# A mixture-of-experts loop: the next expert's gather moved from behind the down projection into it

## The chip, the cores and the metric

The kernel runs on one core of a Trainium2 chip. The metric is the device time of one execution in microseconds (us). All data are float32. TensorE is called PE in the profile, VectorE DVE, ScalarE ACT, GpSimd POOL, SyncE SP.

## The reference, cut to what matters

Two layers over 256 latent tokens of width 1024. The change touches only the last sub-layer, a top-2-of-8 expert SwiGLU (each expert 1024 to 3584 to 1024):

```python
def moe_swiglu(h, router, w_gate, w_up, w_down):
    logits = (h @ router).astype(jnp.float32)
    probs = jax.nn.softmax(logits, axis=-1)
    vals, idx = lax.top_k(probs, TOP_K)
    wts = vals / jnp.sum(vals, axis=-1, keepdims=True)
    combine = jnp.sum(jax.nn.one_hot(idx, N_EXPERTS, dtype=jnp.float32) * wts[..., None], axis=-2)
    ...
    for e in range(N_EXPERTS):
        out = out + combine[..., e:e + 1] * swiglu(h, w_gate[e], w_up[e], w_down[e])
    return out
```

## The kernel before, in words

**Weights.** All weights come as one stream of 2 MB units. SP sends each into one of seven slots of `ring` and waits for the slot's semaphore `used[s]` before it sends the next unit there. An expert has 21 units: 14 for gate and up, 7 for down.

**The loop.** Since 256 tokens choose two experts each, an expert sees only some of them. The kernel picks a padded width for each expert (64, 96, 128, 144, 160, 192 or 256 tokens) from the counts that it finds at run time. The expert loop is a hardware loop (`pe.Fori(0, E)`), and every engine has its own. Inside it, `for_width` is a ladder of if and else on PE: one *arm* of code for each width. The first arm is width 64, and an expert of width 144 passes three branches to reach the fourth. For this input the widths of the eight experts are 64, 96, 144, 64, 128, 64, 96, 64; they can be read from the tiles of the matmuls (64: 128x64 weights, 96: 128x64 and 128x32, 128 and 144: 128 or 144 moving columns at L1186). So there are seven *crossings* from one expert to the next, called crossing 1 to 7 here; crossing 1 is 64 to 96, 2 is 96 to 144, 3 is 144 to 64, 4 is 64 to 128, 5 is 128 to 64, 6 is 64 to 96 and 7 is 96 to 64.

**One expert on PE.** In the arm: `gate_up` (L1204 for widths 64 and 96, L1186 for wider ones; 14 units, banks 0 to 3 of `ps`), then `down` (L1242; 7 units d = 0 to 6, banks 4 to 7). ACT's silu (L419) and DVE's product (L760, which counts `e_a`) make the input of down; for narrow experts it is turned by L1174 and copied by ACT (L412). Behind the arm, in code that all widths share: `gather(e + 1)` (L1135, 16 matmuls, banks 0 to 3) under `pe.If(e < E - 1)` at L1272, which selects the next expert's tokens with a matrix of zeros and ones; then a second ladder with `combine` (L1260), which adds the expert's result to its tokens: 4 matmuls of 512 columns for one block of up to 128 slots (widths 64 and 128), 8 for two blocks (96 and 144). Then the loop's own branch (L1148) goes back to its head, where PE reads the next width and climbs the ladder.

**Around it.** ACT (L437) and DVE (L767) each copy two banks of down's result to `y_slot`, which combine reads; then both take the gathered columns to `hTe` with scale and shift (L402, L747), which the next gate_up reads; DVE adds combine's result to `y_sum` (L773). The last down unit's slot is released by the first gather matmul.

Of the kernel before, what the change touches and what calls it, by code (L numbers as in the profile page):

```python
# [21 lines left out]
P = 128  # L22
# [14 lines left out]
E = 8  # L37
# [4 lines left out]
RING = 7  # L42
UNIT = 4096
BANK = 512
# [39 lines left out]
BASE = len(ORDER)  # L84
# [12 lines left out]
def build(nc, stream, x_in, ctx_in, vecs, consts, rope, dft, gains, ada_b, norm_w, late, out):  # L97
    ctx = ExitStack()
    with ctx:
# [182 lines left out]
        def _(act):  # L282
# [115 lines left out]
            def take_gather(count):  # L398
                for k in range(KD // 2):
                    if k % 2 == 0:  # L400
                        act.wait_ge(gather_ps, count + k // 2 + 1)
                    act.activation(hTe[:, k, :], ps[:, k // 2, (k % 2) * SEQ:(k % 2 + 1) * SEQ], ACT.Identity,  # L402
                                   bias=ab[:, 4, 1, k:k + 1], scale=ab[:, 4, 0, k:k + 1]).then_inc(hTe_act, 1)
# [3 lines left out]
            with act.Fori(0, E) as e:  # L407
                which = act.value_load(width_at[0:1, bass.ds(e, 1)], min_val=0, max_val=len(WIDTHS))

                def take_turned(u):  # L410
                    act.wait_ge(eT_ps, e * GU_UNITS + u + 1)
                    act.activation(aT_e[:, u, :, :].rearrange("p b n -> p (b n)"), ps[:, 6 + u % 2, :],  # L412
                                   ACT.Copy).then_inc(eT_ok, 1)

                def silu_units(wide):
                    for u in range(GU_UNITS):
                        act.wait_ge(e_ps, e * GU_UNITS + u + 1)
                        q = 2 * (u % 2)
                        act.activation(gated_e[:, u % 2, :, :], ps[:, q:q + 2, 0:SEQ], ACT.Silu).then_inc(e_silu, 1)  # L419
                        if u and not wide:  # L420
                            take_turned(u - 1)
                        if u == 5:
                            act.wait_ge(selT_ps, e + 1)
                            act.activation(selT[:, :, :].rearrange("p b t -> p (b t)"), ps[:, 4, :],
                                           ACT.Copy).then_inc(selT_ok, 1)
                    if wide:
                        act.sem_inc(eT_ok, GU_UNITS)
                    else:
                        take_turned(GU_UNITS - 1)

                with act.If(which < WIDE):
                    silu_units(False)
                with act.If(which >= WIDE):
                    silu_units(True)
                act.wait_ge(ye_ps, e + 1)
                for b in range(2):
                    act.activation(y_slot[:, b, 0:BANK], ps[:, 4 + 2 * b, :], ACT.Copy).then_inc(ye_act, 1)  # L437
                with act.If(e < E - 1):
                    take_gather(e * 4 + 4)

            act.activation(stat[:, 127:128], eps[:, 0:1], ACT.Sqrt)

# [10 lines left out]
        def _(dve):  # L453
# [289 lines left out]
            def take_gather(count):  # L743
                for k in range(KD // 2, KD):
                    if k % 2 == 0:
                        dve.wait_ge(gather_ps, count + k // 2 + 1)
                    dve.tensor_scalar(hTe[:, k, :], ps[:, k // 2, (k % 2) * SEQ:(k % 2 + 1) * SEQ],  # L747
                                      ab[:, 4, 0, k:k + 1], ab[:, 4, 1, k:k + 1], ALU.mult,
                                      ALU.add).then_inc(hTe_dve, 1)
# [4 lines left out]
            with dve.Fori(0, E) as e:  # L754
                dve.wait_ge(gather_ps, e * 4 + 4)
                select(e + 1, False)
                for u in range(GU_UNITS):
                    dve.wait_ge(e_silu, e * GU_UNITS + u + 1)
                    q = 2 * (u % 2)
                    dve.tensor_tensor(aT_e[:, u, :, :], gated_e[:, u % 2, :, :], ps[:, q:q + 2, SEQ:2 * SEQ],  # L760
                                      ALU.mult).then_inc(e_a, 1)
                    if u == 7:
                        dve.wait_ge(selT_ps, e + 1)
                        select(e + 1, True)
                dve.wait_ge(ye_ps, e + 1)
                for b in range(2):
                    dve.tensor_copy(y_slot[:, b, BANK:2 * BANK], ps[:, 5 + 2 * b, :]).then_inc(ye_dve, 1)  # L767
                with dve.If(e < E - 1):
                    take_gather(e * 4 + 4)
                for i in range(4):  # L770
                    dve.wait_ge(comb_ps, e * 4 + i + 1)
                    part = y_sum[:, i // 2, (i % 2) * BANK:(i % 2 + 1) * BANK]
                    dve.tensor_tensor(part, part, ps[:, 4 + i, :], ALU.add).then_inc(comb_ok, 1)  # L773
# [12 lines left out]
        def _(pe):  # L786
# [338 lines left out]
                with pe.Else():  # L1125
                    for_width(which, body, i + 1)

            def gather(e, before=None):

                pe.wait_ge(sel_ok, e + 1)
                for j in range(4):
                    for i in range(2):
                        for b in range(TB):
                            last = pe.matmul(ps[:, j, i * SEQ:(i + 1) * SEQ], xn[:, b, (2 * j + i) * P:(2 * j + i + 1) * P],  # L1135
                                             sel[:, b, :], start=(b == 0), stop=(b == TB - 1))
                            if (j, i, b) == (0, 0, 0) and before is not None:
                                last.then_inc(used[before], 1)
                    last.then_inc(gather_ps, 1)

            def landed_of(e, i):
# [6 lines left out]
            with pe.Fori(0, E) as e:  # L1148
# [74 lines left out]
                def down(width):  # L1223
                    pe.wait_ge(selT_ok, e + 1)
                    done, count = done_before(width, GU_UNITS), 0
                    for d in range(NFE // 4):
                        s = landed_of(e, GU_UNITS + d)
                        pe.wait_ge(e_a if is_wide(width) else eT_ok, e * GU_UNITS + 2 * d + 2)
                        w = ring[:, s, :].rearrange("p (f n) -> p f n", f=4)
                        for b, (s0, n) in enumerate(BLOCKS[width]):  # L1230
                            tiles = P // n
                            if d == 0 and b == 1 and not is_wide(width):
                                pe.wait_ge(eT_ok, (e + 1) * GU_UNITS)
                            for h in range(2):
                                for f in range(4):
                                    j, r = 4 * d + f, f % tiles
                                    u = j // 2 if tiles < 4 else 2 * d + 1
                                    c = n * (f % 2 if tiles < 4 else f)
                                    a_T = aT_e[:, u, b, c:c + n]
                                    if is_wide(width):  # L1240
                                        a_T = aT_e[:, j // 2, j % 2, s0:s0 + n]
                                    last = pe.matmul(ps[n * r:n * (r + 1), 4 + 2 * b + h, :], a_T,  # L1242
                                                     w[:, f, h * BANK:(h + 1) * BANK],
                                                     start=(j < tiles), stop=(j >= NFE - tiles))
                                    if count < len(done):
                                        last.then_inc(used[(BASE + done[count]) % RING], 1)
                                    count += 1
                            if d < NFE // 4 - 1 and b == len(BLOCKS[width]) - 1:
                                last.then_inc(used[s], 1)
                            if d == 0 and b == 0 and not is_wide(width):  # L1250
                                turn(width, GU_UNITS - 1)
                    last.then_inc(ye_ps, 1)
                    if is_wide(width):
                        pe.sem_inc(eT_ps, GU_UNITS)

                def combine(blocks):

                    for i in range(4):
                        for b in range(blocks):
                            last = pe.matmul(ps[:, 4 + i, :], selT[:, b, (i // 2) * P:(i // 2 + 1) * P],  # L1260
                                             y_slot[:, b, (i % 2) * BANK:(i % 2 + 1) * BANK],
                                             start=(b == 0), stop=(b == blocks - 1))
                        last.then_inc(comb_ps, 1)

                def expert(width):
# [3 lines left out]
                pe.wait_ge(hTe_act, e * 4 + 4)  # L1269
                pe.wait_ge(hTe_dve, e * 4 + 4)  # L1270
                for_width(width, expert)
                with pe.If(e < E - 1):  # L1272
                    gather(e + 1, (BASE + PER_EXPERT - 1) % RING)
                pe.wait_ge(ye_act, e * 2 + 2)
                pe.wait_ge(ye_dve, e * 2 + 2)
                for_width(width, lambda w: combine(len(BLOCKS[w])))
# [97 lines left out]
```

## Time and profile before

| | before |
|---|---|
| median of 3 runs | 1636.34 us (1633.12 to 1638.41) |
| the profiled execution | 1634.14 us, of which the span is 1632.4 us |
| mean granted clock of TensorE | 0.968 of full speed |
| PE busy | 1524.1 us, 93% of the span |
| DVE, ACT busy | 381.2 us (23%), 266.3 us (16%) |
| moved by DMA | 474.35 MB, mean 291 GB/s |

The span is the time from the first to the last instruction that the profiler recorded; 1.7 us of the execution lie around it. [...] "Issue" in a row is idle time of an engine in which it waited for nothing that the profile shows as work.
### The profile page before, as it was taken

To read this page: it belongs to the slowest core of one execution; us is meant where nothing else is said; L and a number is where in the kernel's file an instruction comes from. 1 tells how busy PE (TensorE), PEld (TensorE's weight loads), DVE (VectorE), ACT (ScalarE), POOL (GpSimd) and SP (SyncE) were. 2 spreads that over 40 slices of the span, in tenths; PEclk is the share of its full clock that TensorE was granted. 3 is DMA by queue.
4 is the path that set the end of the run, shared out by engine and by line. 5 is a ranking of instruction groups with operands and counts; after the bars stand their busy time and mean duration, and the time that the engine had idled before them with its cause. 6 is when DMAs were issued, how large, how long until landed. Compare 5 with 4: busy or idle time off the path is not lost.

```text
span 1632.4 us, 22184 instructions
## 1 busy us (share of the span) xinstructions
PE 1524.1 (93%) x9552; PEld 980.6 (60%) x9553; DVE 381.2 (23%) x663; ACT 266.3 (16%) x506; POOL 16.6 (1%) x18
## 2 busy tenths in 40 slices
PE   5999999999999799799879999996999998999897
PEld 3445598864686464454369954545995564553462
DVE  2668514400265421110010100211010120110212
ACT  3235210001100222121100001221000131120122
POOL 1000010000000000000000000000000000000000
PEclk7999999999999799899989999998999999999999
DMA  9863176842687269889827766798878699889595
GB/s 388 339 255 139 71 291 253 301 187 82 253 316 302 108 283 426 375 339 373 371 75 262 274 244 232 303 428 358 295 287 303 243 428 427 358 350 407 227 428 243
DMA packets 34239, 474.35 MB, mean 291 GB/s; under 512 B 3824, under 2 KB 4112, under 8 KB 5696
## 3 DMA queue, kind: packets, MB, share of 16 engines
q1 hardware_dynamic: 32800, 467.90, 72.2%
q0 software_dynamic: 1024, 3.38, 0.6%
q8 instruction: 120, 1.97, 0.5%
q10 hardware_dynamic: 288, 1.05, 0.2%
q14 instruction: 7, 0.06, 0.0%
HBM read 471.26 MB, written 1.05 MB: 289 GB/s over the span
## 4 chain that ended last, share of the span: by engine, by line
PE 84%; DMA 7%; issue 4%; DVE 4%; ACT 1%; SPq 0%; DVEq 0%
PE ps L1204 22%; PE ps L1186 13%; PE ps L1242 13%; PE ps L997 9%; PE ps L974 8%; DMA ring<-stream 7%; PE ps L1048 5%; PE ps L1135 4%; PE ps L843 3%; PE ps L1260 2%; PE ps L1174 1%; DVE acc L511 1%; DVE att L574 1%; PE ps L945 0%; PE ps L1219 0%
## 5 line engine op out<-in xcount | busy, mean ns | idle before, releaser
L1204 PE MATMUL ps<-ring,hTe 128*64 128x256 f32 (+1 forms) x3584 | 361.8, 384 | 11.3 <-issue 9.9
L1204 PEld LDWEIGHTS ps<-ring,hTe 128*64 128x64 f32 (+1 forms) x3584 | 216.6, 131 | 134.4 <-issue 27.3
L1242 PE MATMUL ps<-ring,aT 128*64 128x512 f32 (+2 forms) x1232 | 286.7, 597 | 7.9 <-DMA ring<-stream 6.4
L1186 PE MATMUL ps<-hTe,ring 128*128 128x144 f32 (+1 forms) x1792 | 215.2, 284 | 20.9 <-issue 20.9
L1186 PEld LDWEIGHTS ps<-hTe,ring 128*128 128x128 f32 x1792 | 214.6, 194 | 22.7 <-issue 22.7
L1242 PEld LDWEIGHTS ps<-ring,aT 128*64 128x64 f32 (+2 forms) x1232 | 96.2, 139 | 188.0 <-issue 170.7
L760 DVE TENSOR_TENSOR aT<-hT,ps 128x512 f32<-128x512 f32 x112 | 77.0, 687 | 548.0 <-ACT hT L419 548.0
L419 ACT ACTIVATE hT<-ps 128x512 f32<-128x512 f32 x112 | 66.9, 597 | 569.5 <-PE ps L1204 337.1
L997 PE MATMUL ps<-hT,ring 128*128 128x256 f32 (+1 forms) x832 | 153.4, 347 | 0.0
L997 PEld LDWEIGHTS ps<-hT,ring 128*128 128x128 f32 x832 | 138.1, 191 | 15.7 <-issue 1.0
L511 DVE SCALAR_TENSOR_TENSOR acc<-ring,silu_c,acc 128x1024 f32<-128x1024 f32 (+1 forms) x92 | 105.2, 1143 | 2.0
L974 PE MATMUL ps<-ring,aT 128*128 128x512 f32 x240 | 104.5, 594 | 0.0
L1135 PE MATMUL ps<-acc,xn 128*128 128x256 f32 x256 | 68.3, 433 | 23.4 <-issue 20.7
L1048 PE MATMUL ps<-hT,ring 128*128 128x256 f32 (+1 forms) x480 | 83.9, 337 | 0.0
L1048 PEld LDWEIGHTS ps<-hT,ring 128*128 128x128 f32 x480 | 76.2, 191 | 7.9 <-issue 0.5
L1135 PEld LDWEIGHTS ps<-acc,xn 128*128 128x128 f32 x256 | 56.0, 222 | 38.6 <-issue 26.6
L974 PEld LDWEIGHTS ps<-ring,aT 128*128 128x128 f32 x240 | 45.1, 190 | 56.2 <-issue 56.2
L767 DVE COPY acc<-ps 128x512 f32<-128x512 f32 x16 | 10.3, 686 | 286.4 <-PE ps L1242 286.4
L412 ACT ACTIVATE aT<-ps 128x512 f32<-128x512 f32 x84 | 49.8, 593 | 18.2 <-PE ps L1174 18.2
L437 ACT ACTIVATE acc<-ps 128x512 f32<-128x512 f32 x16 | 8.7, 594 | 257.0 <-PE ps L1242 257.0
L843 PE MATMUL ps<-ring,hT 128*128 128x512 f32 x96 | 43.1, 610 | 1.3 <-DVE hT L498 1.3
L1260 PE MATMUL ps<-acc 128*128 128x512 f32 x88 | 39.2, 593 | 1.6 <-DVE acc L767 1.6
(180 smaller groups left out, 705.1 us busy)
## 6 DMA issues: line engine op xcount, KB each, us to landing
ring<-stream SPq DMA_DIRECT2D x222, 2048.0 KB, 11.1
gg<-norm_w POOLq DMA_DIRECT2D x4, 512.0 KB, 14.8
x<-x_in SPq DMA_DIRECT2D x1, 1024.0 KB, 5.1
hTe<-ctx_in SPq DMA_DIRECT2D x1, 1024.0 KB, 7.9
out<-x ACTq DMA_DIRECT2D x2, 512.0 KB, 2.6
aT<-dft POOLq DMA_DIRECT2D x1, 512.0 KB, 10.8
aT<-rope POOLq DMA_DIRECT2D x1, 256.0 KB, 15.4
acc<-late POOLq DMA_DIRECT2D x1, 192.0 KB, 2.7
```

The lines of the kernel that those rows point to most:

```text
L419: act.activation(gated_e[:, u % 2, :, :], ps[:, q:q + 2, 0:SEQ], ACT.Silu).then_inc(e_silu, 1)
L511: last = dve.scalar_tensor_tensor(out=dst, in0=slot(what)[:, k * D:(k + 1) * D][:, cols], scalar=silu_c[:, 4 * h + k, 0:1], in1=dst, op0=A ...
L760: dve.tensor_tensor(aT_e[:, u, :, :], gated_e[:, u % 2, :, :], ps[:, q:q + 2, SEQ:2 * SEQ], ALU.mult).then_inc(e_a, 1)
L843: last = pe.matmul(ps[:, blk, :], lhs[:, k, b * P:(b + 1) * P], w[:, k, :], start=(k == 0), stop=(k == KD - 1))
L974: last = pe.matmul(ps[:, 4 + 2 * b + h, :], lhs(k)[:, b * P:(b + 1) * P], w[:, k % per_unit, h * BANK:(h + 1) * BANK], start=(k == 0), sto ...
L997: last = pe.matmul(ps[:, j % 4, g * SEQ + t0:g * SEQ + t1], w[:, j % 2, g, k, :], hT[:, k, t0:t1], start=(k == 0), stop=(k == KD - 1))
L1048: last = pe.matmul(ps[:, bank, c + t0:c + t1], w[:, i % 4, k, :], hT[:, k, t0:t1], start=(k == 0), stop=(k == KD - 1))
L1135: last = pe.matmul(ps[:, j, i * SEQ:(i + 1) * SEQ], xn[:, b, (2 * j + i) * P:(2 * j + i + 1) * P], sel[:, b, :], start=(b == 0), stop=(b = ...
L1186: last = pe.matmul(ps[:, 2 * (u % 2) + b, g * SEQ:g * SEQ + width], w, hTe[:, k, 0:width], start=(k == 0), stop=(k == KD - 1))
L1204: last = pe.matmul(to, hTe[:, k, s0:s0 + n], w, start=(k == 0), stop=(k == KD - 1))
L1242: last = pe.matmul(ps[n * r:n * (r + 1), 4 + 2 * b + h, :], a_T, w[:, f, h * BANK:(h + 1) * BANK], start=(j < tiles), stop=(j >= NFE - tiles))
L1260: last = pe.matmul(ps[:, 4 + i, :], selT[:, b, (i // 2) * P:(i // 2 + 1) * P], y_slot[:, b, (i % 2) * BANK:(i % 2 + 1) * BANK], start=(b = ...
```

## The change

On PE the gather of expert e+1 leaves the shared code. It stands now in each of the seven arms, in `down`, behind the fourth unit (d = 3), under an if of its own that skips it for the last expert. There it waits until all 14 products of the expert are made (`e_a`), since it writes banks 0 to 3. On ACT and DVE the taking of the gathered columns (`take_gather`) goes ahead of the copies of down's result. The slot of the last down unit is now released by the first matmul of combine; so that this comes early, combine's first group of 512 columns is split into 128 and 384.

```diff
@@ ACT (act) @@
+                with act.If(e < E - 1):
+                    take_gather(e * 4 + 4)
                 act.wait_ge(ye_ps, e + 1)
                 for b in range(2):
                     act.activation(y_slot[:, b, 0:BANK], ps[:, 4 + 2 * b, :], ACT.Copy).then_inc(ye_act, 1)
-                with act.If(e < E - 1):
-                    take_gather(e * 4 + 4)
@@ DVE (dve) @@
+                with dve.If(e < E - 1):
+                    take_gather(e * 4 + 4)
                 dve.wait_ge(ye_ps, e + 1)
                 for b in range(2):
                     dve.tensor_copy(y_slot[:, b, BANK:2 * BANK], ps[:, 5 + 2 * b, :]).then_inc(ye_dve, 1)
-                with dve.If(e < E - 1):
-                    take_gather(e * 4 + 4)
@@ PE, down(width) @@
+                        if d == 3:
+                            with pe.If(e < E - 1):
+                                pe.wait_ge(e_a, (e + 1) * GU_UNITS)
+                                gather(e + 1)
                     last.then_inc(ye_ps, 1)
@@ PE, combine(blocks) @@
-                        for b in range(blocks):
-                            last = pe.matmul(ps[:, 4 + i, :], selT[:, b, (i // 2) * P:(i // 2 + 1) * P],
-                                             y_slot[:, b, (i % 2) * BANK:(i % 2 + 1) * BANK],
-                                             start=(b == 0), stop=(b == blocks - 1))
+                        half = slice((i % 2) * BANK, (i % 2 + 1) * BANK)
+                        for part in ([slice(0, P), slice(P, BANK)] if i == 0 else [slice(0, BANK)]):
+                            for b in range(blocks):
+                                last = pe.matmul(ps[:, 4 + i, part], selT[:, b, (i // 2) * P:(i // 2 + 1) * P],
+                                                 y_slot[:, b, half][:, part], start=(b == 0), stop=(b == blocks - 1))
+                                if part.stop == P and b == 0:
+                                    last.then_inc(used[(BASE + PER_EXPERT - 1) % RING], 1)
                         last.then_inc(comb_ps, 1)
@@ PE, the loop @@
                 for_width(width, expert)
-                with pe.If(e < E - 1):
-                    gather(e + 1, (BASE + PER_EXPERT - 1) % RING)
                 pe.wait_ge(ye_act, e * 2 + 2)
                 pe.wait_ge(ye_dve, e * 2 + 2)
                 for_width(width, lambda w: combine(len(BLOCKS[w])))
```

How it stands in the program, on PE at the end of the arm for width 64 (a name like `ps<-ring,aT` is output and inputs; the line number of a row may shift by two to three between the kernels). Before:

```order
L1242 MATMUL ps<-ring,aT 64x512 x40
L1123 UNCONDITIONAL_BRANCH
L1123 COMPARE_AND_BRANCH
L1143 ISA
L1204 MATMUL ps<-ring,hTe 64x2x128 x32
```

And of the change:

```order
L1240 MATMUL ps<-ring,aT 64x512 x16
L1251 COMPARE_AND_BRANCH
L1252 REGISTER_ALU
L1131 REGISTER_ALU
L1135 MATMUL ps<-acc,xn 128x256 x16
L1251 UNCONDITIONAL_BRANCH
L1240 MATMUL ps<-ring,aT 64x512 x24
L1123 UNCONDITIONAL_BRANCH
```

The last 40 down matmuls were one run; now 24 of them follow the gather, and the arm's exit branch follows them as before.

On PE behind the ladder, where the exit branch of every arm leads. Before:

```order
L1272 COMPARE_AND_BRANCH
L1131 REGISTER_ALU
L1135 MATMUL ps<-acc,xn 128x256 x16
L1272 UNCONDITIONAL_BRANCH
L1274 ISA
L1123 COMPARE_AND_BRANCH
L1260 MATMUL ps<-acc 128x512 x4
L1123 UNCONDITIONAL_BRANCH
L1123 COMPARE_AND_BRANCH
L1260 MATMUL ps<-acc 128x512 x8
```

The same place of the change, down to the end of combine's ladder and the loop's branch:

```order
L1125 UNCONDITIONAL_BRANCH
L1277 ISA
L1123 COMPARE_AND_BRANCH
L1264 MATMUL ps<-acc 128x128
L1264 MATMUL ps<-acc 128x384
L1264 MATMUL ps<-acc 128x512 x3
L1123 UNCONDITIONAL_BRANCH
...
L1125 UNCONDITIONAL_BRANCH
L1146 REGISTER_ALU
L1146 COMPARE_AND_BRANCH
```

Between the arm's exit and combine's ladder there were 16 matmuls; now there is none. Combine's seven arms stand between its first branch and the loop's branch in both.

On ACT behind the silu units, before:

```order
L437 ACT_TABLE_LOAD
L437 ACTIVATE acc<-ps 128x512 x2
L438 COMPARE_AND_BRANCH
L401 REGISTER_ALU
L402 ACTIVATE hTe<-ps,ab 128x256 x2
```

And of the change:

```order
L402 ACTIVATE hTe<-ps,ab 128x256 x2
L435 UNCONDITIONAL_BRANCH
L437 REGISTER_ALU
L439 ACT_TABLE_LOAD
L439 ACTIVATE acc<-ps 128x512 x2
```

The columns are taken first, and the copies stand last.

## Rows read from the trace of the kernel before

**Rows 1.** The page, part 5: the gather and combine on PE
```profile
L1135 PE MATMUL ps<-acc,xn 128*128 128x256 f32 x256 | 68.3, 433 | 23.4 <-issue 20.7
...
L1260 PE MATMUL ps<-acc 128*128 128x512 f32 x88 | 39.2, 593 | 1.6 <-DVE acc L767 1.6
```
**Rows 2.** Waits of PE, 560 to 1632: waiting line, releaser, total us, times, longest
```profile
PE ps L1186 <- issue: 20.9, 2, 10.9
...
PE ps L1204 <- issue: 9.9, 3, 3.9
PE ps L1242 <- DMA ring<-stream: 6.4, 6, 1.3
```
**Rows 3.** The chain around crossing 1: start us, us, what
```profile
660.89 3.07 issue
663.96 8.86 PE ps L1135 x32
672.82 3.43 PE ps L1260 x8
676.25 3.86 issue
680.11 13.46 PE ps L1204 x128
```
**Rows 4.** The chain at crossings 2, 3, 4, 5 and 7
```profile
802.74 5.02 issue
...
823.87 10.91 issue
...
1010.44 1.83 issue
...
1106.77 2.62 issue
...
1121.44 9.98 issue
...
1282.54 6.91 PE ps L1135 x32
...
1516.22 5.26 issue
```
**Rows 5.** Branches at L1123, ns min/median/max, starts: crossings 1 and 4, last expert
```profile
L1123 PEldq COMPARE_BRANCH  x5: 66/257/6287, 657.3 to 679.9; - x5
L1123 PEldq COMPARE_BRANCH  x6: 66/323/6234, 1103.2 to 1131.2; - x6
L1123 PEldq COMPARE_BRANCH  x3: 66/1596/3402, 1614.4 to 1619.6; - x3
```
**Rows 6.** The loop's branch (L1148) at crossings 1, 2, 3 and 5
```profile
L1148 PEldq COMPARE_BRANCH  x1: 7433/7433/7433, 671.1 to 671.1; - x1
L1148 PEldq COMPARE_BRANCH  x1: 3343/3343/3343, 816.8 to 816.8; - x1
L1148 PEldq COMPARE_BRANCH  x1: 4679/4679/4679, 1019.2 to 1019.2; - x1
L1148 PEldq COMPARE_BRANCH  x1: 6419/6419/6419, 1287.5 to 1287.5; - x1
```
**Rows 7.** DMA queues in 661 to 662, then in 667 to 668: packets, MB, share
```profile
q8 instruction: 1, 0.02, 6.6%
q8 instruction: 1, 0.02, 6.9%
```
**Rows 8.** The last expert's end, timeline: DVE's copies and combine
```profile
1618.02 1.29 DVE L767 COPY acc<-ps 128x512 f32<-128x512 f32 x2 [25.38 <-PE ps L1242]
...
1619.58 3.69 PE L1260 MATMUL ps<-acc 128*128 128x512 f32 x8 [1.60 <-DVE acc L767]
```
**Rows 9.** Windows around crossing 1: us, busy by engine, PEclk, DMA share, GB/s
```profile
664.00:668.00 4.00, 4.00 (x12) 3.30 (x13) 0.00 (x0) 1.02 (x2) 0.00 (x0) 0.65 1.00 422
680.00:686.00 6.00, 5.89 (x30) 3.44 (x32) 0.00 (x0) 0.00 (x0) 0.00 (x0) 0.53 1.00 423
```

More of the change, by code:

```diff
@@ L1126, in for_width, with gather @@
                     for_width(which, body, i + 1)
-            def gather(e, before=None):
+            def gather(e):
                 pe.wait_ge(sel_ok, e + 1)
@@ L1136, in gather @@
                                              sel[:, b, :], start=(b == 0), stop=(b == TB - 1))
-                            if (j, i, b) == (0, 0, 0) and before is not None:
-                                last.then_inc(used[before], 1)
                     last.then_inc(gather_ps, 1)
```

## The prediction

> **What bounds the kernel now.** I read the page first: PE is busy nearly all the time, and gather and combine, which stand at the seven crossings between experts, take 68.3 and 39.2 us of it [rows 1]. The first gather (9.5 us) lies ahead of the loop, and the last combine takes 3.7 us [rows 8], so the crossings hold 58.8 us of gather and 35.5 us of combine. Next the waits of PE: it idles 20.7 us ahead of gathers [rows 1] and 20.9 + 9.9 us ahead of the next expert's gate_up [rows 2], always on "issue", that is on nothing that another engine does. A crossing, from the last down matmul to the next expert's first, thus costs all seven together 20.7 + 58.8 + 35.5 + 30.8 = 145.8 us. Third, the chain shows the shape: 3.07 idle, gather, combine, 3.86 idle [rows 3]; at crossing 2 it is 5.02 and 10.91 [rows 4].
>
> What the idle is, the branches of PE's sequencer tell. The arm's exit at crossing 1 starts at 657.3 and takes 6.29 us, to 663.6 [rows 5]; the gather starts at 663.96 [rows 3]. In that time the instruction queue moves a packet, and another 6 us later [rows 7]: code is being brought in. The sequencer runs ahead of the array: the exit is taken 3.6 us before down ends. So also for the loop's branch. It starts at 671.1, that is 1.7 us **before** combine's first matmul (672.82), takes 7.43 us, and 1.6 us after its end the next expert starts, at 680.11 [rows 3, 6]. Combine and half of the gather lay over it. This is the point of the whole case: a gather of 7 to 9 us stands where the sequencer has two loads of code to wait for, and it covers them. Of the idle that can be seen, the code loads are only what sticks out.
>
> **The change part by part.**
>
> *The gather in the arm.* It costs there 16 matmuls at full clock, 6.91 us at crossing 5, where no idle lies ahead of it [rows 4], seven times: +48.3 us. What it may hide: the narrow arms wait in down for weights, 6.4 us in all [rows 2], of which 1.2 at the last expert, which makes no gather; a PE that comes later waits less, so -5.2. The array is otherwise busy in down. Net **+43.1 us**. The wait on `e_a` costs nothing: three units of down lie over the last product. The taking of columns on ACT and DVE now lies under units 4 to 6 of down; nothing is queued behind it there but the wait for down's end. Combine's split adds one small group; its price has no row, is between nothing and 0.3 us a crossing, and I take nothing.
>
> *The crossing without the gather.* Now the order is: exit load, copies of down's result, combine, loop branch. The copies end 1.3 us after down and combine starts 1.56 us after it at the last expert [rows 8]; every exit but crossing 5's is idle 1.83 us or longer [rows 3, 4], so they are exposed at crossing 5 alone. What counts is the chain of loads. The code behind the exit comes in pieces: at the last expert the exit ends at 1617.8, and the branch behind combine stands still for 1.60 us until 1621.2 [rows 5], 3.4 us after the first piece, with no weights on the move; with weights on the move the two packets are 6.0 us apart [rows 7]. Before, the gather lay over this second piece; now the loop's branch cannot be taken before it. Then the loop's branch itself, and 1.6 us to the first matmul. With weights on the move (crossings 1, 4, 6):
>
> - Crossing 1: exit 2.7 after down's end, second piece 6.0, loop's branch 7.4, head 1.6: 17.7 us.
> - Crossing 4: exit 2.3, 6.0, 7.3, and the head with the ladder's branch of 6.2 us [rows 5]: 7.9; 23.5 us. Crossing 6 is like 1, 17.4 us.
>
> With the queue mostly empty (2, 3, 5, 7) the second piece is 3.4, and the loop's branch took 3.3, 4.7 and 6.4 [rows 6]. It will meet the last slot's unit, now released at the same moment by combine, so I take 5.5:
>
> - Crossing 3: exit 1.6, 3.4, 5.5, head 1.5: 12.0 us. Crossing 7: exit 3 (between 1.5, where copies end, and its 5.26 [rows 4]; in a longer arm the DMA queue is emptier), 3.4, 5.5, 1.5: 13.4 us.
> - Crossing 2: exit 3, 3.4, 5.5, and from the loop's branch (816.8 + 3.3 = 820.1) to the first matmul at 834.7 14.6 us, since three branches of the ladder are loads [rows 4, 6]: 26.5 us.
> - Crossing 5: copies 1.6, ladder and issue 1.2, 5.5, 1.5: 9.8 us.
>
> In all 120.3 us, against 145.8 before: **-25.5 us**. Taking 58.8 us of gather away buys no more than that, for the idle grows from 51.5 us to some 85.
>
> *The clock.* [...] Crossings 3, 5 and 7 have little or no idle ahead of gate_up now and get 5 us or more: each 0 to 2.8 us, I take 1.3: **+4 us**.
>
> Sum: 43.1 - 25.5 + 4 = +21.6 us on the profiled execution's 1634.1, which is 2.2 us under the median: 1636.3 + 21.6 = **1658 us**.
>
> [...]
>
> **The rivals.**
>
> *The second piece is there in time* (chance 0.09). Then 3 x 5.5 and 3 x 2.9 us fall away: -25 us, 1633 us, no change. For it: behind other branches pieces came while PE worked. Against: there was a gather to work on, and where there was none it showed [rows 5].
>
> *The branches keep their whole length* (0.10). The time from the gather's start to the next expert (16.2 us at crossing 1 [rows 3]) stays, though the gather is gone. Then the 43.1 come on top of an unchanged crossing: 1679 us. For it: at crossings 1, 2, 4, 5 and 6 the loads, not the array, end last. Against: there the sequencer also had to wait for room behind the gather's matmuls.
>
> *The gather's place was the cost* (0.07), the other sign. If the idle ahead of the next expert does not grow, 30.8 us, the crossing loses its 58.8 us and gains 1.6 at crossing 5: -57.2 + 43.1 = -14 us, less the slow clock that passes from gather to combine (58.8 - 48.4 = 10.4 at most, 4 likely): 1626 us. It decides if the loop's branch ends no later after combine's first matmul than now, 5.7 us at crossing 1 (678.5 - 672.8). For it: the exit load does cover the copies. Against: the branch was asked for 1.7 us ahead of combine, and nothing is left ahead of which it could be asked for.
>
> **How the numbers follow.** A measurement here tells 0.3%, 4.9 us, from no change. The forecast has 0.74, its own range 1647 to 1670: 3.4 instead of 6.0 for the three pieces and 4.7 for the four light branches below, 7.3 for those and 2.8 for each clock above. With rivals in, 1638 to 1674. Slower: 0.74 + 0.10 and a little of the first rival, 0.85; same 0.07; faster 0.08.
>
> **What would show it.** Right: gathers at some 6.9 us each inside the arms at full clock, no waits for weights in the units behind them; combine starting 1.6 to 3.1 us after down; the loop's branch starting 5 us or more **after** combine's first matmul at crossings 1, 4 and 6; idle on issue ahead of gate_up grown from 30.8 to about 65 to 75 us, at all seven crossings; the branch behind combine long (3 us or more with weights on the move). Wrong: that branch at 0.2 to 0.4 us (first rival); or idle ahead of gate_up no larger than before (third). What would break the sum is another path of the branches, such as code still present from a pass before, or a loop branch of 3.3 us everywhere.

## The result, and the profile after

The changed kernel takes 1659.46 us (median of 4 runs, 1658.04 to 1662.23) against 1635.12 us of the kernel before on the same chip: a ratio of 1.0149, 95% interval [1.0126, 1.0172]. It is slower by 24 us. The forecast was 1658 us. The profiled execution has a span of 1657.1 us, 24.7 more than before.

The page of the changed kernel, parts 1 and 5. They answer to the share of PE in the table of before and to [rows 1]:

```profile
PE 1521.5 (92%) x9574; PEld 978.6 (59%) x9575; DVE 381.6 (23%) x663; ACT 275.2 (17%) x513; POOL 16.6 (1%) x18
...
L1264 PE MATMUL ps<-acc 128*128 128x512 f32 (+2 forms) x110 | 47.1, 589 | 22.1 <-issue 12.4
L1135 PE MATMUL ps<-acc,xn 128*128 128x256 f32 x256 | 59.7, 393 | 2.7 <-DVE acc L740 2.7
```

PE works 2.6 us less than before and the kernel is 24.7 us longer, so all of it is idle. The gathers (L1135) fell from 68.3 to 59.7 us, and no loop gather is preceded by idle any more: each of the seven takes 7.1 to 7.2 us, where five took 8.6 to 9.2 us before. Combine (now L1264) grew from 39.2 to 47.1 us. Nearly all of that is at four crossings, where it stands behind the exit's idle and the granted clock fell, as it did in the gathers before: at crossings 2, 3 and 7 it takes 8.8, 8.8 and 9.2 us (clock 0.81, 0.81 and 0.77; 7.0 us each before), at crossing 4 5.4 us (0.68; 3.6 before). At crossings 1, 5 and 6 and at the last expert the clock in it is 1.00 and it takes 3.7 us. At the three crossings that is 0.1 us more than before, about what the split adds.

PE's waits from 560 us on, which answer to [rows 2] (line, releaser, total us, times, longest):

```profile
PE ps L1184 <- issue: 32.6, 2, 16.5
PE ps L1202 <- issue: 29.7, 5, 11.1
PE ps L1264 <- issue: 12.4, 3, 4.9
PE ps L1264 <- DVE acc L769: 9.7, 5, 2.2
...
PE ps L1240 <- DMA ring<-stream: 1.2, 1, 1.2
```

Idle ahead of the next expert's gate_up (L1184, L1202) doubled, from 30.8 us at five crossings to 62.3 us at all seven. Waits for weights in down fell from 6.4 to 1.2 us, as forecast.

The chain around crossing 1, to be laid beside [rows 3]:

```profile
663.83 0.55 issue
...
665.64 3.70 PE ps L1264 x10
669.35 11.08 issue
```

Combine starts 1.9 us after down's end, since the exit's branch (659.3 + 6.0) now ends 1.5 us after it, where it ended 2.7 us after it before; but behind combine's 3.7 us PE stands for 11 us. The branches of PE's sequencer say why. First the exit and the branch behind combine (L1123, starts 659.3 and 665.7; the middle value of the three is the latter), then the loop's branch (L1146), both at crossing 1; then the loop's branch at crossings 3 and 7:

```profile
L1123 PEldq COMPARE_BRANCH  x3: 79/5616/5958, 659.3 to 665.7; - x3
L1146 PEldq COMPARE_BRANCH  x1: 7296/7296/7296, 671.5 to 671.5; - x1
...
L1146 PEldq COMPARE_BRANCH  x1: 8007/8007/8007, 1027.0 to 1027.0; - x1
L1146 PEldq COMPARE_BRANCH  x1: 7591/7591/7591, 1553.3 to 1553.3; - x1
```

The branch behind combine, a jump of 0.39 us in the kernel before, stands still for 5.6 us. The loop's branch starts 5.8 us after combine's first matmul, where it started 1.7 us ahead of it [rows 3, 6], and takes 7.3 us, where it took 7.4. At crossings 3 and 7 it takes 8.0 and 7.6 us, where it took 4.7 and 3.4 before; at crossing 2 it is 7.6 where it was 3.3.

### The profile page after: what moved, and what is told of

It reads as the page before. It is cut to its first block, busy times and chain, and to the rows that moved or that the text cites. A ratio compares the mean times of both kernels' runs of the same rounds, so it can differ in the third digit from the quotient of the medians.

```text
span 1657.1 us, 22240 instructions
## 1 busy us (share of the span) xinstructions
PE 1521.5 (92%) x9574; PEld 978.6 (59%) x9575; DVE 381.6 (23%) x663; ACT 275.2 (17%) x513; POOL 16.6 (1%) x18
## 4 chain that ended last, share of the span: by engine, by line
PE 86%; issue 5%; DVE 4%; DMA 3%; ACT 1%; SPq 0%; DVEq 0%
PE ps L1202 22%; PE ps L1240 16%; PE ps L1184 13%; PE ps L997 9%; PE ps L974 8%; PE ps L1048 5%; PE ps L1135 4%; PE ps L843 3%; DMA ring<-stream 3%; PE ps L1264 3%; PE ps L1172 1%; DVE acc L511 1%; DVE att L574 1%; PE ps L945 0%; PE ps L1217 0%
## 5 line engine op out<-in xcount | busy, mean ns | idle before, releaser
L1202 PE MATMUL ps<-ring,hTe 128*64 128x256 f32 (+1 forms) x3584 | 362.1, 385 | 31.1 <-issue 29.7
L1202 PEld LDWEIGHTS ps<-ring,hTe 128*64 128x64 f32 (+1 forms) x3584 | 216.9, 131 | 154.4 <-issue 47.4
L1184 PE MATMUL ps<-hTe,ring 128*128 128x144 f32 (+1 forms) x1792 | 216.3, 285 | 32.6 <-issue 32.6
L1184 PEld LDWEIGHTS ps<-hTe,ring 128*128 128x128 f32 x1792 | 215.6, 195 | 34.4 <-issue 34.4
L1264 PE MATMUL ps<-acc 128*128 128x512 f32 (+2 forms) x110 | 47.1, 589 | 22.1 <-issue 12.4
L1135 PE MATMUL ps<-acc,xn 128*128 128x256 f32 x256 | 59.7, 393 | 2.7 <-DVE acc L740 2.7
L747 DVE TENSOR_SCALAR hTe<-ps,ab 128x256 f32<-128x256 f32 x32 | 15.9, 539 | 194.3 <-PE ps L1135 194.3
L1135 PEld LDWEIGHTS ps<-acc,xn 128*128 128x128 f32 x256 | 49.8, 197 | 15.1 <-issue 5.4
L1264 PEld LDWEIGHTS ps<-acc 128*128 128x128 f32 x110 | 22.4, 230 | 47.2 <-issue 46.2
```

The lines of the kernel that those rows point to most:

```text
L1184: last = pe.matmul(ps[:, 2 * (u % 2) + b, g * SEQ:g * SEQ + width], w, hTe[:, k, 0:width], start=(k == 0), stop=(k == KD - 1))
L1202: last = pe.matmul(to, hTe[:, k, s0:s0 + n], w, start=(k == 0), stop=(k == KD - 1))
L1264: last = pe.matmul(ps[:, 4 + i, part], selT[:, b, (i // 2) * P:(i // 2 + 1) * P], y_slot[:, b, half][:, part], start=(b == 0), stop=(b == ...
```

## The experiments

All ratios are to the kernel before, run on the same chip. e1 to e4 were run together, and so were e5 to e8 and e9 to e11; the kernel before had medians of 1634.71, 1636.62 and 1633.63 us in these three sets and 1633.82 in that of e12, so differences of one or two us between sets say nothing.

| kernel | median us | ratio, interval |
|---|---|---|
| e1: changed, 8 matmuls more at each crossing | 1660.36 | 1.0160 [1.0135, 1.0185] |
| e2: changed, 16 more | 1675.33 | 1.0254 [1.0229, 1.0280] |
| e3: changed, ACT and DVE order undone | 1660.06 | 1.0158 [1.0133, 1.0184] |
| e4: changed, short combine ladder | 1625.14 | 0.9941 [0.9921, 0.9961] |
| e5: changed, slot released late | 1654.83 | 1.0110 [1.0094, 1.0127] |
| e6: before, short combine ladder | 1635.77 | 1.0002 [0.9985, 1.0019] |
| e7: e6 and tree of widths | 1624.01 | 0.9928 [0.9909, 0.9947] |
| e8: e4 and tree of widths | 1619.61 | 0.9890 [0.9872, 0.9908] |
| e9: e4, code moved by 80 instructions | 1649.51 | 1.0085 [1.0052, 1.0119] |
| e10: e4, code moved by 16 | 1625.19 | 0.9929 [0.9905, 0.9954] |
| e11: e6, code moved by 128 | 1621.27 | 0.9919 [0.9893, 0.9945] |
| e12: e7, code moved by 128 | 1613.30 | 0.9874 [0.9851, 0.9897] |

### e1 and e2: work at the crossing

```diff
                 for_width(width, expert)
+                with pe.If(e < E - 1):
+                    pe.wait_ge(hTe_act, e * 4 + 8)
+                    pe.wait_ge(hTe_dve, e * 4 + 8)
+                    for n in range(8):    # e2: 16
+                        pe.matmul(ps[:, n % 4, 0:SEQ], xn[:, 0, (n % 8) * P:(n % 8 + 1) * P], sel[:, 0, :],
+                                  start=True, stop=True)
```

> The changed kernel with 8 further matmuls of 256 columns (results unused, banks 0 to 3) behind the arm's exit and ahead of combine, at each of the seven crossings. They are 3.5 us of work each, 24 us in all. Theory (the crossing is a chain of code loads, and work laid over them is free): at crossings 1, 4 and 6 they lie under the second piece of code, which the branch behind combine waits 5.2 to 5.6 us for; at the others a part shows, so +0 to +10 us, 1659 to 1669. Rival (the crossing costs what its work costs, and the loss of the change is the 16 matmuls that the arm now holds plus exposed copies): +24 us, 1683.

> The same with 16 matmuls, as many as the gather has: 7 us of work each, 49 us in all. Theory: the crossing becomes what it was before the change, 145 us for all seven instead of 125, so +20 us (15 to 28), about 1680. Rival (work costs its own time): +49 us, 1708.

Against the 1659.46 us of the changed kernel (from another set of runs), 24 us of added work cost 1 us, and 49 us cost 16; both are as forecast. The chain of e1 around crossing 1 (L1281 is the added work):

```profile
663.79 2.02 issue
665.81 3.69 PE ps L1281 x16
669.50 3.44 PE ps L1264 x10
672.95 7.57 issue
```

From down's end to the next expert it is 16.7 us, as without the work (16.6), and the idle is shorter by as much as was put in. The rival, that a crossing costs what its matmuls cost, is out. Of 16 matmuls at this place, as many as the gather has, two thirds (33 of 49 us) do not show in the time. Not all of this is cover for the second piece of code. At crossings 2, 3 and 7 the loop's branch of e1 takes 5.4, 4.2 and 5.6 us, where the changed kernel has 7.6, 8.0 and 7.6: with the added work ahead of combine the sequencer asks for the branch within 0.2 us of the last slot's 2 MB unit, and not 1.3 to 1.9 us behind it. e5 comes back to this unit.

### e3: the order on ACT and DVE

```diff
-                with act.If(e < E - 1):
-                    take_gather(e * 4 + 4)
                 act.wait_ge(ye_ps, e + 1)
                 ...
+                with act.If(e < E - 1):
+                    take_gather(e * 4 + 4)
```

and the same on DVE.

> The changed kernel with one part undone: on ACT and DVE the copies of down's result come first again, and the gathered columns are taken behind them. The gather stays in the arm. Theory: PE's chain of branches does not depend on it, and the taking (some 2.2 us) ends well ahead of the next expert's first matmul, 8.9 us or more after down at every crossing: 0 us, 1657 to 1662. Rival (the order on ACT and DVE costs, for the copies that combine waits for stand last in their queues): 3 us or more faster.

It measured 1660.06 us: this half of the change does nothing for the time.

### e4: a shorter way from the exit to the loop's branch

```diff
-                for_width(width, lambda w: combine(len(BLOCKS[w])))
+                with pe.If(width == 0):
+                    combine(1)
+                with pe.Else():
+                    with pe.If(width == 2):
+                        combine(1)
+                    with pe.Else():
+                        combine(2)
```

> The changed kernel with combine's ladder of seven arms replaced by three (width 64, width 128, all others), which take the code between the arm's exit and the loop's branch from some 256 instructions to some 90. The same matmuls run. Theory: the branch behind combine no longer waits for a second piece of code; it was long at all crossings but 5 (5.6, 1.9, 1.5, 5.6, 5.2 and 2.1 us), so 12 to 24 us fewer, 1635 to 1647. Rival (the second piece is not what the crossing waits for; the load of the loop's head takes its place in the queue, or the waits for the copies bound it): within 5 us of the changed kernel, 1655 to 1664.

It won 34 us, more than the theory's 12 to 24, and is faster than the kernel before. In its trace, all branches of combine's ladder (L1279), the loop's branches (L1146) and PE's waits ahead of gate_up:

```profile
L1279 PEldq COMPARE_BRANCH  x12: 73/193/257, 669.6 to 1614.6; - x12
...
L1146 PEldq COMPARE_BRANCH  x8: 76/3854/6906, 670.1 to 1615.0; - x8
...
PE ps L1184 <- issue: 18.5, 2, 11.5
...
PE ps L1202 <- issue: 8.2, 3, 3.6
```

The 5.6 us branch is gone: none takes over 0.26 us. The surplus is in the loop's branches. Their median fell from 7.4 (in the changed kernel) to 3.9 us: at crossings 2, 3, 5 and 7 they start 0.2 to 0.3 us ahead of the last slot's unit, with no other unit on the move, and take 3.4 to 3.9 us.

### e5: when the last slot is released

```diff
-                        for part in ([slice(0, P), slice(P, BANK)] if i == 0 else [slice(0, BANK)]):
+                        for part in ([slice(0, P), slice(P, BANK)] if i == 3 else [slice(0, BANK)]):
```

> The changed kernel with the slot of the last down unit released in combine's last group of columns instead of its first (the group that is split moves too), 3 us later for one block and 6 us for two. In the changed kernel the loop's branch takes 7.6, 8.0 and 7.6 us at crossings 2, 3 and 7, where it took 3.3, 4.7 and 3.4 before, and its two packets of code move only some 4 us after it starts, when that slot's 2 MB unit has been sent. Theory (code waits behind this unit): 3 to 4 us fewer at each of the three, nothing at the others, where units move anyway: 6 to 12 us faster, 1648 to 1654. Rival (the branch is longer for another reason, as that it now asks for two packets): 1657 to 1663.

4.6 us faster than the changed kernel, measured in another set of runs (by the ratios, 1.0110 and 1.0149, 6.4 us; the intervals just touch). The loop's branch at crossings 3 and 7:

```profile
L1146 PEldq COMPARE_BRANCH  x1: 4626/4626/4626, 1027.2 to 1027.2; - x1
L1146 PEldq COMPARE_BRANCH  x1: 4616/4616/4616, 1550.6 to 1550.6; - x1
```

8.0 and 7.6 us became 4.6. In the changed kernel the 2 MB unit goes out 1.3 and 1.9 us ahead of these two branches, in e5 5.4 and 4.7 us behind their start: the load of code had waited for the unit. The rival would have left them long. The size is at or under the lower end of the forecast, because after 4.6 us combine itself ends last at these two crossings (PE has no idle ahead of gate_up there), and because crossing 2 gained nothing: its loop's branch fell as well, from 7.6 to 4.6 us, but the next branch, in the ladder of widths, rose from 3.8 to 6.7 us. It starts at 822.3, and the unit now goes out at 821.5, just ahead of it. So that crossing shows the same effect once more.

### e6 to e8: the same ladder in the kernel before, and a tree of widths

e6 is e4's edit in the kernel before. e7 and e8 add this to e6 and to e4:

```diff
-                with pe.If(which == i):
-                    body(WIDTHS[i])
-                with pe.Else():
-                    for_width(which, body, i + 1)
+                def split(lo, hi):
+                    if hi - lo == 1:
+                        body(WIDTHS[lo])
+                        return
+                    mid = lo + 1 if hi - lo < 4 else (lo + hi) // 2
+                    with pe.If(which < mid):
+                        split(lo, mid)
+                    with pe.Else():
+                        split(mid, hi)
+                split(0, len(WIDTHS))
```

> The kernel before with the short combine ladder (three arms for seven), gather at its old place behind the arm. Theory: the gather already lies over the second piece of code, so there is less to win than the 35 us that the changed kernel won, but the loop's branch no longer has a third piece asked for just ahead of its own at crossings 1, 3, 4, 5 and 6: 5 to 20 us faster than before, 1615 to 1630. Rival (the gain of the short ladder is independent of the gather's place): 1600.

> The same, and the ladder over the widths made a tree (first question: one of the three narrowest or not; then on by halves), so that width 144 is reached with one branch to far code instead of three. Theory: at crossing 2 two of three loads of 4.6 to 4.7 us go: 8 to 10 us faster than e6 (e6 less 9). Rival (the loads of the ladder overlap with something else): the same as e6.

> The changed kernel with both, short combine ladder and tree. In the changed kernel with the short ladder crossing 2 still had one branch of 6.4 and one of 4.5 us in the widths' ladder. Theory: one of them goes, 4 to 7 us faster than the 1625 us of the short ladder alone, 1618 to 1621; and it stays slower than e7, since there the gather works while code comes. Rival: the gather's place no longer matters once the ladders are short, e8 equals e7 within 3 us.

e6 won nothing, and both of its expectations miss. e7 won 12 us over e6, a little more than forecast: the tree does save loads at crossing 2, where the widths' ladder has one branch of 4.1 us in e7 and had three of 4.0, 4.7 and 5.1 us in e6. e8 won 5.5 us over e4, as expected, but is 4 us faster than e7 and not slower, so that part of the expectation falls, and with it the plain form of my theory, "the gather is worth more where code loads can hide behind it". Something separated e6 from e4 that I had not counted. e9 to e11 look for it: where the border between two pieces of code falls. (A piece is what one packet of the instruction queue brings: 122 packets carry 2.00 MB in the changed kernel, 16.4 KB each. How many instructions that is can be counted in the arm of width 144 of the kernel before: the queue brings packets at 900.9, 916.3, 932.0, 948.0 and 982.8 us, and between the first and the last stand 511 records of PE and 513 of PEld, 256 instructions for each of the four steps.)

### e9 to e11: the same instructions at another place

```diff
                 def expert(width):
+                    if width == WIDTHS[-1]:
+                        for _ in range(20):    # e10: 4, e11: 32
+                            pe.matmul(ps[:, 0, 0:P], ident, ident, start=True, stop=True)
```

The arm of width 256 is never taken with this input. The way of which the texts speak is the one from the arm's exit to the loop's branch.
> The changed kernel with the short combine ladder (e4), and 20 matmuls more in the arm of width 256, which no expert takes: not one instruction more runs. [...]
> The control for it: 4 such matmuls that never run, 16 instructions, which should leave all of that way within one piece. Theory: as e4, 1622 to 1629. If any shift costs, for a reason other than the border, it is slower.

> The kernel before with the short combine ladder (e6, which won nothing) and 32 matmuls that never run in the arm of width 256. In e6 the border of a piece should still fall between gather and the loop's branch; 128 instructions on, gather, combine and the loop's branch should lie in one piece. Theory: the loop's branch is no longer behind a third piece, 6.4 us become some 3.6 at crossing 5, and 7.4 some 6.6 at 1, 4 and 6, and what the changed kernel won at crossing 2 (one header less to load) may come too: 4 to 15 us faster than e6, 1620 to 1632. Rival (under the gather all of it was covered already): 1636.

e9 lost 24 us against e4, and against e10 of its own set, by instructions that never run; e10 lost none. e11 won 14 us over e6. Below are all branches of combine's ladder, then the loop's, first of e9 (L1282, L1146), then of e6 (L1276, L1148), then of e11 (L1279, L1148):

```profile
L1282 PEldq COMPARE_BRANCH  x12: 73/244/5759, 667.2 to 1634.7; - x12
L1146 PEldq COMPARE_BRANCH  x8: 76/6231/7712, 672.8 to 1636.6; - x8
```

```profile
L1276 PEldq COMPARE_BRANCH  x12: 66/242/1502, 667.6 to 1619.1; - x12
L1148 PEldq COMPARE_BRANCH  x8: 76/5104/7597, 669.6 to 1620.8; - x8
```

```profile
L1279 PEldq COMPARE_BRANCH  x12: 66/200/248, 665.8 to 1604.9; - x12
L1148 PEldq COMPARE_BRANCH  x8: 76/4322/6504, 667.6 to 1605.3; - x8
```

With the border between exit and loop branch (e9, e6, and the changed kernel) a branch of combine's ladder shows a wait of 5.76, 1.50 and 5.6 us, and the loop's branch goes to 7.6 us or more. Without it (e4, e10, e11) the ladder's longest is 0.26 us and the loop's longest 6.9. In e6 the gather covered the ladder's branch, so only the last expert shows it, but the loop's branch was still long. The packets say the same. From the start of the exit to the start of the loop's branch the instruction queue moves two at crossings 1, 4 and 6 of e9 and one in e10; during the loop's branch at crossings 1, 4, 5 and 6 it moves two in e6 and one in e11.

How the border costs differs from crossing to crossing. At crossings 1, 4 and 6 of e9 a branch of combine's ladder waits 5.2 to 5.8 us. At 2, 3 and 7 none does, but the loop's branch comes 1.2 to 1.7 us behind the last slot's unit, and takes 6.2, 5.8 and 6.3 us, against 3.9, 3.7 and 3.6 in e10, where it comes ahead of the unit.

The traces hold a difference that the border does not explain. At crossing 2 the middle one of the three branches in the widths' ladder took 4.6 to 5.0 us in the kernel before, the changed one and e6, but 0.2 us in e4, e9, e10 and e11. Of the 14 us that e11 won over e6, 4.4 are this branch; the loop's branches at crossings 1, 4, 5 and 6 give another 4.7. No run changed this branch alone, so why it needs no load there stays open.

This orders the gather's place too. With a border on the way, the place behind the arm is better by 13.7 us (e6, 1635.77, against e9, 1649.51, from two sets of runs; ratios 1.0002 and 1.0085). Without one it is better by 4 us in the medians (e11, 1621.27, against e10 of the same set, 1625.19, and e4, 1625.14), which the intervals of the ratios, [0.9893, 0.9945], [0.9905, 0.9954] and [0.9921, 0.9961], do not separate. That e8 beat e7 fits: only e7 had the border. Its longest branch in combine's ladder takes 1.64 us (at the last expert) and its longest loop's branch 7.7; in e8 they take 0.26 and 6.8. Without the border the old place has the lower median again (e12, below, 1613.30 against e8's 1619.61), but the intervals of these two overlap as well.

### e12: a version that beats both

> The version that the runs so far point to: the kernel before (gather behind the arm) with the short combine ladder, the widths' ladder as a tree (both as in e7), and the 32 matmuls that never run of e11, so that gather, combine and the loop's branch lie in one piece of code. Theory: the two gains add, e11's 14 us under e6 and e7's 12 us under e6: 1636 - 26 = 1610 us (1606 to 1616), faster than the kernel before and than the changed kernel with short ladder and tree (1620). Rival (they share what they save): 1620.

1613.30 us, ratio 0.9874, 20.5 us under the kernel before, 46 us under the changed one, and within the forecast. The two gains add for the larger part: 22.5 us under e6, where 26 were forecast (1.28% of 1.57% by the ratios). They share the middle branch of crossing 2: the tree saves 9.6 us of ladder branches there in e7, and 4.8 us in e12 against e11, where that branch no longer cost anything. Its waits of PE ahead of gather (L1138) and gate_up (L1189, L1207):

```profile
PE ps L1138 <- issue: 20.3, 6, 5.0
PE ps L1189 <- issue: 10.2, 2, 8.9
PE ps L1207 <- issue: 6.4, 3, 2.8
```

30.8 us ahead of gate_up became 16.6. The 20.3 us of the arms' exits are untouched.

## Why the prediction was right, step by step

The change made the kernel 24.3 us slower; 21.6 were forecast. The mechanism was the one that the runs show. That the time itself came within 2 us is in part luck: of the terms below, the first two came out 1.8 and 5.9 us above the forecast and the third 2.6 us below it.

- **The gather in the arm, +48.3 - 5.2.** Measured: the seven take 59.7 less 9.57 for the first, 50.1 us, since six of them take 7.1 us in the chain and not 6.91, and since busy time counts each some 0.1 us longer than the chain, from which 6.91 was read; waits for weights fell by just 5.2. 44.9 instead of 43.1.
- **The crossing without the gather, -25.5.** Measured: idle 62.3 ahead of gate_up, 22.1 - 1.6 (the last expert) ahead of combine, combine 47.1 - 3.7; in all 126.2 us against 145.8, -19.6, 5.9 less than forecast. The mechanism held: the branch behind combine waits for its second piece, the loop's branch comes 5.8 us after combine's start, and the whole idle is 82.8 us, where some 85 were forecast (ahead of gate_up 62.3, a little under the 65 to 75). The copies are exposed at crossings 1, 4, 5 and 6 and not at 5 alone, since the exits of 1, 4 and 6 ended sooner than before; that made these crossings shorter, not longer. With weights on the move the sizes were right: 16.6 us at crossing 1 where 17.7 were forecast, 23.4 at 4 (23.5), 16.2 at 6 (17.4). The mis-sized term is the loop's branch with the queue mostly empty, for which I took 5.5 us: it took 7.6, 8.0 and 7.6 us at crossings 2, 3 and 7 and 4.9 at 5. The text named the cause, the last slot's unit, and took too little for it; e5 shows that it is this unit. A smaller miss is the exit at 2 and 7, taken at 3 us behind down: it ended 3.9 and 4.1 us behind it.
- **The clock, +4.** It rests on 2.8 us for a slow start of an expert, the author's estimate from the 6 us at a granted clock of 0.53 in [rows 9]; no run shows that price by itself. What the trace of the changed kernel shows in its place: L1202 and L1184 together are busy 1.4 us longer than their lines before. The slow clock went to combine instead, which takes 7.6 us more at crossings 2, 3, 4 and 7. These 7.6 us are within the 126.2 above; PE stands idle behind combine for 2.4 to 16.5 us there, so they lie over the sequencer's waits. Sum by these figures: 44.9 - 19.6 + 1.4 = +26.7, against a span longer by 24.7; most of the rest is that the loop began 1.6 us earlier in this execution (its first gather at 566.70; 568.26 before).
- **The first rival** (second piece in time) is refuted by the 5.6 us branch.
- **The second rival** (branches keep their whole length, 1679 us) fell in the sum, but was near the truth where loads alone end last: the time from the first matmul behind the exit to the next expert shrank only from 16.2 us to 14.8 at crossing 1, from 27.0 to 25.3 at 2, from 22.0 to 21.5 at 4 and from 15.9 to 14.2 at 6. Most of what the change won at the crossings came at 3, 5 and 7 (14.0 to 11.2, 12.7 to 6.8 and 16.0 to 11.8). What the prediction held against it, the sequencer's wait for room behind the gather, fits the trace of before: at all seven crossings 15 or 16 records of PE (matmuls) have still to start ahead of the next expert when the loop's branch starts. **The third** (idle does not grow) fell: it doubled.

Not tried: whether part of the idle at the exits would go if the units were sent so that none is on the move when an arm ends.

## What to carry to other kernels

In a loop with branches, work behind a branch may be covering the load of the code that comes next. Before moving it, read the sequencer's branches (which start, how long) beside the array's rows, and ask when the next branch could be asked for without that work. Then keep the way between two far branches short and within one piece of code (e9 against e10: 24 us), and climb long ladders of if and else by halves: that won 1.3% here, where moving 59 us of work off the crossings lost 1.5%.

## What the runs showed of the hardware that was not expected

- Twenty matmuls that never run, standing in an arm that is not taken, cost 24 us (e9, 1649.51 us, against e10, 1625.19, and e4, 1625.14), 3.5 us a crossing in the mean.
- A load of code waited for weight transfers that were issued just ahead of it. At crossings 2, 3 and 7 the loop's branch took 3.5 to 3.9 us in e4, where it came ahead of the 2 MB unit, 4.6 in e5, where the unit went out later still, and 7.6 to 8.0 us in the changed kernel, where the unit went 1.3 to 1.9 us ahead of it.
- Not every branch to far code was a load: the ladder's branch to the arm of width 96 took 0.26 us right after the arm of width 64 had run (the median of the first line of [rows 5]). That fits code which was still there from the end of that arm, some 20 us before. At crossing 2, after the longer arm of width 96, the same branch took 3.8 us. No run tests this apart.
